# Seven block products in place of eight for the gate and up matrices of a decoder step's feed-forward layers

## The reference, cut to what matters

```python
def swiglu(x, w_gate, w_up, w_down):
    return (jax.nn.silu(x @ w_gate) * (x @ w_up)) @ w_down
...
f1 = swiglu(rmsnorm(x, W['ffn1_pre_g'][l]), W['ffn1_w_gate'][l], W['ffn1_w_up'][l], W['ffn1_w_down'][l])
x = x + 0.5 * rmsnorm(f1, W['ffn1_post_g'][l])
```

## Time and profile before

| | us |
|---|---|
| median of 3 runs | 1166.08 |
| lowest, highest | 1164.78, 1174.18 |
| span of the profiled execution, first to last instruction | 1167.8 |
| its PE busy | 1120.6 |
| its DVE busy | 615.3 |
| its ACT busy | 329.2 |
| its POOL busy | 42.9 |

### The profile page before, as it was taken

How to read it: one execution, slowest core, us unless ns; L and a number is a source line. 1 busy time by engine, 2 the same in 40 slices (tenths; PEclk the granted TensorE clock), 3 DMA queues, 4 the chain that set the end, 5 groups by cost and what they waited for, 6 DMA issues and landing times. The chain is left out here.

```text
span 1167.8 us, 22671 instructions
## 1 busy us (share of the span) xinstructions
PE 1120.6 (96%) x9522; PEld 1097.9 (94%) x9522; DVE 615.3 (53%) x1015; ACT 329.2 (28%) x496; POOL 42.9 (4%) x57
## 2 busy tenths in 40 slices
PE   6999999999999999999899989999999999999996
PEld 6999999999999999999777789999999999999996
DVE  5534344323434778788869637873434333243446
ACT  5321222112222334331234433442122221122221
POOL 0000000000000000030223000000000000000001
PEclk9999999999999979999779989899999999999998
DMA  6322323222232221232601002213232322222222
GB/s 216 95 80 90 108 72 103 78 90 91 72 108 72 73 86 38 63 88 60 96 2 39 2 1 93 73 41 95 77 113 72 108 72 90 90 82 98 72 73 77
DMA packets 35394, 91.99 MB, mean 79 GB/s; under 512 B 10368, under 2 KB 12928, under 8 KB 35328
## 3 DMA queue, kind: packets, MB, share of 16 engines
q1 hardware_dynamic: 34320, 88.78, 25.0%
q10 hardware_dynamic: 1008, 2.27, 0.6%
HBM read 87.76 MB, written 3.28 MB: 78 GB/s over the span
## 5 line engine op out<-in xcount | busy, mean ns | idle before, releaser
L306 PE MATMUL ps<-xh,wh 128*128 128x272 f32 x1840 | 404.0, 293 | 16.4 <-DVE xl L503 8.6
L306 PE MATMUL ps<-xh,wl 128*128 128x272 f32 x1840 | 400.3, 291 | 0.0
L306 PE MATMUL ps<-xl,wh 128*128 128x272 f32 x1840 | 399.3, 290 | 0.0
L306 PEld LDWEIGHTS ps<-xh,wh 128*128 128x128 f32 x1840 | 299.3, 191 | 19.0 <-DVE wl L289 9.0
L306 PEld LDWEIGHTS ps<-xl,wh 128*128 128x128 f32 x1840 | 299.6, 191 | 0.0
L306 PEld LDWEIGHTS ps<-xh,wl 128*128 128x128 f32 x1840 | 297.7, 191 | 0.0
L284 ACT ACTIVATE wh<-raw 128x1024 fp32r<-128x1024 f32 (+1 forms) x163 | 168.1, 1034 | 324.6 <-PE ps L306 208.6
L289 DVE TENSOR_TENSOR wl<-raw,wh 128x1024 fp32r<-128x1024 f32 (+1 forms) x163 | 192.8, 1203 | 38.0 <-ACT wh L284 37.7
L306 PE MATMUL ps<-hh,wh 128*128 128x272 f32 x704 | 157.7, 290 | 0.0
L306 PE MATMUL ps<-hh,wl 128*128 128x272 f32 x704 | 156.7, 290 | 0.0
L306 PE MATMUL ps<-hl,wh 128*128 128x272 f32 x704 | 156.5, 289 | 0.0
(11 more groups left out here) (312 smaller groups left out, 790.3 us busy)
## 6 DMA issues: line engine op xcount, KB each, us to landing
raw<-in_w_gu SPq DMA_DIRECT2D x88, 512.0 KB, 3.6
raw<-in_w_d SPq DMA_DIRECT2D x32, 512.0 KB, 3.6
raw<-in_w_in SPq DMA_DIRECT2D x19, 512.0 KB, 3.6
raw<-in_w_d SPq DMA_DIRECT2D x16, 384.0 KB, 3.0
raw<-in_w_out SPq DMA_DIRECT2D x8, 512.0 KB, 3.6
out_y<-x SPq DMA_DIRECT2D x16, 136.0 KB, 1.7
x<-in_x ACTq DMA_DIRECT2D x4, 272.0 KB, 5.6
x<-in_x SPq DMA_DIRECT2D x4, 272.0 KB, 6.7
```

The lines of the kernel that those rows point to most:

```text
L306: last = pe.matmul(out[:, n], left[:, s, j], right[:, j, n * H:n * H + H], start=first and opens and j == order[0], stop=final and closes ...
```

## The change

In groups 1 and 2 of both feed-forward layers (16 of the 22 hidden tiles in each) the gate and up units of a hidden tile are replaced by seven block products. The weights of a tile are taken as a 2 x 2 matrix of blocks (gate and up, by first and second half of the contraction), the input as another (first and second half of the contraction, by first and second half of the tokens). Of a 2 x 2 block product, seven products of sums of blocks do instead of eight (the Winograd form). Each of the seven is 4 x 3 = 12 matmuls of 272 columns.

What is added around them:

- Per feed-forward layer, during the down product of group 0: for four pairs of input tiles, ACT copies them times the norm's gain (`rows_act`, two of 544 columns), GpSimd makes four sums of 272 columns (`ffn_pool`), ACT and DVE split these into `seven` (`rows_hi_act`, `rows_lo_dve`, 1088 columns each).
- Per hidden tile: GpSimd makes four sums of weight blocks of 512 columns (`fast_pool`), in the columns of `xh` and `xl` that the seven products don't read. ACT and DVE split seven blocks instead of four half tiles' worth of two units (`fast_hi`, `fast_lo`: three of 512 columns and two of 1024). The products add up in three PSUM banks of 272 columns; between them ACT copies a partial sum out four times (`fast_copy`), and the next product adds on in the same bank. DVE joins the parts with three additions of 272 columns (`fast_first`, `fast_gate`), multiplies by `rb`, and after silu multiplies twice by 272 columns (`fast_hidden`); the hidden tile's split is as before.
- A second load buffer `raw2` holds the odd tiles; a tile's two loads (gate and up) are issued together, when the tile two before it is split.

The same 2 x 512 KB per hidden tile are loaded. Group 0, the down products and the mixer keep their instructions; the counters of both layers are merged and the units renumbered.

```diff
+        seven = at("ffn", "seven", [2, 4, 4, H], F32R, offset=TB)
+        raw2 = at("ffn", "raw2", [2, KD, P], offset=TB + 32 * 4 * H)
...
+        def fast_sp(sp, q, g, u):
+            f0, nf = GROUPS[g]
+            with sp.Fori(0, nf // 2) as i:
+                for s in range(2):
+                    sp.wait_ge(S("f_lo"), i * 10 + (5 * (16 * q + f0 - FAST0 + s) + 5))
+                    if s:
+                        sp.wait_ge(S("q_lo"), 4 * q + 4)
+                    else:
+                        sp.wait_ge(S("w_lo"), u + RAW)
+                    for k in range(2):
...
+                        sp.dma_start(fast_raw(s, k).rearrange("p k n -> p (k n)"), src).then_inc(S(f"f_raw{s}"), 16)
+
+        def fast_pool(pool, q, g):
...
+                    landed(pool, q, g, i, s)
+                    pool.wait_ge(S("f_lo"), i * 10 + (5 * n + 7))
+                    pool.tensor_tensor(sum_(0), up[:, 0:4], up[:, 4:8], ADD).then_inc(S("f_sum"), 1)
+                    pool.wait_ge(S("f_sum"), i * 8 + (16 * q + 16 + 4 * n + 1))
+                    pool.tensor_tensor(sum_(1), sum_(0), gate[:, 0:4], SUB).then_inc(S("f_sum"), 1)
+                    pool.wait_ge(S("f_lo"), i * 10 + (5 * n + 9))
+                    pool.tensor_tensor(sum_(2), gate[:, 0:4], up[:, 0:4], SUB).then_inc(S("f_sum"), 1)
+                    pool.wait_ge(S("f_sum"), i * 8 + (16 * q + 16 + 4 * n + 2))
+                    pool.tensor_tensor(sum_(3), gate[:, 4:8], sum_(1), SUB).then_inc(S("f_sum"), 1)
...
+        def fast_pe(pe, q, g, i, s, dn):
...
+            for m, (high, low) in enumerate(rights):
+                pe.wait_ge(S("f_lo"), i * 10 + (10 + 5 * n + (1, 2, 2, 3, 4, 4, 5)[m]))
+                if m == 1:
+                    pe.wait_ge(S("q_lo"), 4 * q + 4)
+                if m in (2, 4, 5, 6):
+                    pe.wait_ge(S("f_copy"), i * 8 + (4 * n + {2: 1, 4: 3, 5: 2, 6: 4}[m]))
+                out = fast_bank(s, (0, 1, 0, 2, 0, 1, 0)[m])
+                hi, lo_ = slots(wh, m), slots(wl, m)
+                for j in range(4):
+                    for left, right in ((hi, high), (hi, low), (lo_, high)):
+                        last = pe.matmul(out, left[:, j], right[:, j], start=m in (0, 1, 3) and j == 0 and left is hi and right is high,
+                                         stop=j == 3 and left is lo_, skip_group_check=True)
+                last.then_inc(S("f_done"), 1)
...
+        def fast_gate(dve, q, g, i, s):
...
+            dve.tensor_tensor(h32[:, s % 2, H:N], h32[:, s % 2, H:N], five[s % 2][:], ADD).then_inc(S("f_part"), 1)
+            dve.wait_ge(S("f_done"), i * 14 + (7 * (n + 1) + 6))
+            dve.tensor_tensor(silu[:, s % 2, H:N], fast_bank(s, 1), silu[:, s % 2, H:N], ADD).then_inc(S("f_part"), 1)
+            dve.wait_ge(S("f_part"), i * 6 + (3 * n + 3))
+            dve.tensor_tensor(silu[:, s % 2], silu[:, s % 2], rb[:], MUL).then_inc(S("gate"), 1)
+
+        def fast_hidden(dve, q, g, i, s):
...
+            dve.tensor_tensor(h32[:, s % 2, H:N], silu[:, s % 2, H:N], h32[:, s % 2, H:N], MUL)
...
+            dve.tensor_tensor(h32[:, s % 2, 0:H], silu[:, s % 2, 0:H], fast_bank(s, 0), MUL).then_inc(S("h_mul"), 1)
+            hidden_split_dve(dve, q, i, f0, s)
+
+        def fast_tile_act(act, q, g, i, s):
+            fast_copy(act, q, g, i, s, 0)
+            fast_hi(act, q, g, i, s + 1, 0)
+            fast_copy(act, q, g, i, s, 1)
+            fast_copy(act, q, g, i, s, 2)
+            fast_hi(act, q, g, i, s + 1, 1)
+            fast_hi(act, q, g, i, s + 1, 2)
+            fast_copy(act, q, g, i, s, 3)
+            fast_hi(act, q, g, i, s + 1, 3)
+            silu_act(act, q, i, GROUPS[g][0], s)
+            fast_hi(act, q, g, i, s + 1, 4)
+
+        def fast_tile_dve(dve, q, g, i, s):
+            fast_lo(dve, q, g, i, s + 1, 0)
+            fast_lo(dve, q, g, i, s + 1, 1)
+            fast_first(dve, q, g, i, s)
+            fast_lo(dve, q, g, i, s + 1, 2)
+            fast_gate(dve, q, g, i, s)
+            fast_lo(dve, q, g, i, s + 1, 3)
+            fast_hidden(dve, q, g, i, s)
+            fast_lo(dve, q, g, i, s + 1, 4)
...
+                pool.tensor_tensor(qq[:, 0], b12, b11, SUB).then_inc(done, 1)
+                pool.tensor_tensor(qq[:, 2], b22, b12, SUB).then_inc(done, 1)
...
                 for s in range(KD):
...
                     split_hi(act, u, 0, s, nf)
                     if s == 1:
                         silu_act(act, q, 0, f0, nf - 1)
...
+                    if s % 2 == 0:
+                        if s:
+                            rows_hi_act(act, q, s // 2 - 1)
+                        rows_act(act, q, s // 2)
+                rows_hi_act(act, q, 3)
```

More of the change, by code:

```diff
@@ L262, in program @@
         block = ctx.enter_context(nc.Block())
-        FFN_UNITS = sum(2 * nf + KD for _, nf in GROUPS)
+        FFN_UNITS = 2 * GROUPS[0][1] + KD * len(GROUPS)
         MIX0 = FFN_UNITS
@@ L713, in final_pool, with fast_raw, slots, two @@
                 pool.tensor_tensor(x[:, k, part_of(1)], x[:, k, part_of(1)], tb3[:, k % 3, part_of(1)], ADD).then_inc(S("y_pool"), 1)
+        FAST0 = GROUPS[1][0]
+        def fast_raw(s, k):
+            return (raw2 if s % 2 else raw)[:, k]
+        def slots(w, first, count=1):
+            return w[:].rearrange("p s k n -> p (s k) n")[:, 4 * first:4 * (first + count)]
+        def two(t):
+            return t.rearrange("p (s k) n -> p s k n", s=2)
+        def sum_(n):
+            return sums[n // 2][:, :, H + P * (n % 2):H + P * (n % 2) + P]
@@ new lines, in fast_pool @@
+        def fast_pool(pool, q, g):
+            f0, nf = GROUPS[g]
+            with pool.Fori(0, nf // 2) as i:
+                for s in range(2):
+                    n = 16 * q + f0 - FAST0 + s
+                    gate, up = fast_raw(s, 0), fast_raw(s, 1)
+                    landed(pool, q, g, i, s)
[7 more added lines that the diff above has]
+                    pool.tensor_tensor(sum_(3), gate[:, 4:8], sum_(1), SUB).then_inc(S("f_sum"), 1)
@@ new lines, in fast_hi @@
+        def fast_hi(act, q, g, i, s, k, u=None):
+            n = 16 * q + GROUPS[g][0] - FAST0 + s
+            if k in (1, 3):
+                act.wait_ge(S("f_sum"), i * 8 + (16 * q + 16 + 4 * n + k + 1))
+            else:
+                landed(act, q, g, i, s)
+            act.wait_ge(S("f_done"), i * 14 + (7 * n + (1, 3, 4, 6, 7)[k]))
+            if u is not None:
+                act.wait_ge(S("unit_done"), SPL + u - 4 + (1, 2, 2, 3, 4)[k])
+            act.activation(left_to(wh, k), left_of(s, k), ACT.Copy).then_inc(S("f_hi"), 1)
@@ new lines, in fast_copy @@
+        def fast_copy(act, q, g, i, s, k):
+            f0 = GROUPS[g][0]
+            n = 16 * q + f0 - FAST0 + s
+            act.wait_ge(S("f_done"), i * 14 + (7 * (n + 1) + (1, 2, 3, 5)[k]))
+            if k == 0:
+                act.wait_ge(S("h_mul"), i * 2 + (FT * q + f0 + s + 1))
+            if k == 3:
+                act.wait_ge(S("h_lo"), i * 2 + (FT * q + f0 + s + 1))
+            to = (silu[:, s % 2, 0:H], five[s % 2][:], silu[:, s % 2, H:N], h32[:, s % 2, H:N])[k]
+            act.activation(to, fast_bank(s, (0, 1, 0, 0)[k]), ACT.Copy).then_inc(S("f_copy"), 1)
@@ new lines, in slots_free, with fast_act @@
+        def slots_free(act, q, g, s):
+            f0, nf = GROUPS[g]
+            act.wait_ge(S("f_done"), 7 * (16 * q + f0 - FAST0 + nf) + (2, 4, 6, 7)[s])
+            act.wait_ge(S("h_mul"), FT * q + f0 + nf - 1 + 1)
+        def fast_act(act, q, g, u):
+            f0, nf = GROUPS[g]
+            for k in range(5):
+                fast_hi(act, q, g, 0, 0, k, u)
+            with act.Fori(0, nf // 2 - 1) as i:
+                for s in range(2):
+                    fast_tile_act(act, q, g, i, s)
+            fast_tile_act(act, q, g, nf // 2 - 1, 0)
+            end = (q, g, nf // 2 - 1, 1)
+            fast_copy(act, *end, 0)
+            fast_copy(act, *end, 1)
+            for d in range(4):
+                if d in (1, 2):
+                    fast_copy(act, *end, d + 1)
+                if d == 3:
+                    silu_act(act, q, nf // 2 - 1, f0, 1)
+                slots_free(act, q, g, d)
+                split_hi(act, u, 0, d, nf)
@@ new lines, in fast_dve @@
+        def fast_dve(dve, q, g, u, n):
+            f0, nf = GROUPS[g]
+            for k, d in enumerate((4, 5, None, 6, 7)):
+                fast_lo(dve, q, g, 0, 0, k)
+                if d and (g > 1 or d > 5):
+                    down_dve(dve, q, u - KD, g - 1, d, n)
+            with dve.Fori(0, nf // 2 - 1) as i:
+                for s in range(2):
+                    fast_tile_dve(dve, q, g, i, s)
+            fast_tile_dve(dve, q, g, nf // 2 - 1, 0)
+            end = (q, g, nf // 2 - 1, 1)
+            split_lo(dve, u, 0, 0, nf)
+            fast_first(dve, *end)
+            split_lo(dve, u, 0, 1, nf)
+            fast_gate(dve, *end)
+            split_lo(dve, u, 0, 2, nf)
+            fast_hidden(dve, *end)
```

(25 more changed lines are left out.)

185 lines of the change are left out of this document (137 added, 48 removed).

## The result

| | before | after |
|---|---|---|
| median (lowest to highest), 17 runs each, us | 1174.16 (1164.78 to 1179.81) | 1162.69 (1153.68 to 1166.33) |
| ratio, 95% interval | | 0.9907, 0.9886 to 0.9929 |
| span of the profiled execution | 1167.8 | 1152.4 |
| feed-forward stages, groups 1 and 2 of the first layer, then of the second | 96.2, 96.2, 96.2, 96.2 | 95.5, 88.6, 95.3, 88.7 |

The account below looks back on a forecast made before the run. PE was taken as the bound, the number of matmuls setting the stages' time. 1167.8 - 47.4 saved + 6 of standing PE = 1126.4 against the profiled span, 1.7 above the runs' median: 1125 us, range 1117 to 1154.

Parts of the forecast that it names:

- Matmuls: 32 hidden tiles go from 96 to 84 matmuls, 12.03 to 10.55 us each, saving 47.4 us (46.4 to 48.3).
- the lower of the two ends: New hidden tile on PE: 10.52 us at the 0.1252 pitch, the other end 10.58 at 0.1259.
- The price of a sum: Hidden tiles: each 512-column GpSimd sum costs DVE 0.85 us (0 to 1.13), on top of 8.3 a tile alone.
- the bounds given: GpSimd's weight sums were to take 1.1 to 1.9 us each, stretched by turns with DVE.
- The group's budget: Eight-tile group: DVE needs 86.8 us beside PE's 84.4; PE stands 1.5 per group, 6 in all (0 to 32).
- the cushion: Within a tile's chain of gate, silu and copy, DVE may be 1.2 us late before PE stands.
- The input sums: Beside group 0's down units: 27 us of work hidden, counted as nothing; uncovered, at most some 10 us twice.
- The sum: Whole kernel: 1167.8 - 47.4 + 6 = 1126.4 against the profiled span, so 1125 us.
- A: Rival, the port: GpSimd and DVE hardly overlap, 24 tiles with sums take 11.2 to 12.8 us; 1154 us, chance 0.21.
- C: Rival, the copies: products wait for ACT to empty their PSUM bank, 19 us lost; 1144 us, chance 0.12.
- B: Rival, the clock: PE stands in each of 24 tiles and its clock falls; 1177 to 1226, named 1195 us, chance 0.06.

Follow-up runs that it names:

- e5: Changed kernel with DVE instead of GpSimd making the weight sums, and DVE's input-sum low parts moved ahead of down outputs: 1132.09 us, 0.9645 of before.
- e1: Changed kernel with GpSimd's weight sums cut from 512 columns to one, except in group 1's first two tiles: 1141.82 us, 0.9746 of before.
- e3: Changed kernel with DVE's low parts of the input sums moved ahead of the down outputs in group 0: 1153.3 us, 0.9843 of before.
- e6: Changed kernel with one-column weight sums (except group 1's first two tiles) plus four unread 512-column GpSimd sums per tile: 1195.51 us, 1.0201 of before.
- e4: Changed kernel with a tile's first PSUM copy on ACT moved ahead of the previous tile's silu and last split: 1159.72 us, 0.9872 of before.

## Why the prediction was wrong

**Matmuls, right.** 9138 of them; without waits a tile takes 10.50 us (e5), just under the lower of the two ends, so twelve matmuls into one bank cost nothing beyond the pitch.

**The price of a sum, right.** A tile of DVE was put at 8.3 alone and 0.85 a sum, 11.7 with four; it measures 11.62. The two terms are off by a little, in opposite directions: alone it is 8.04 (e5), so a sum costs (11.62 - 8.04) / 4 = 0.9. That 8.3 and 0.85 give nearly the same total is luck. The stretched operations say the same: 1.11 lost by the 272 columns, 0.50 by the cast, 0.88 by `hl`, 1.08 by the two low parts (2.37 against 1.29 in e1), 3.57 in all. POOL's sums take 1.35 to 1.69 us on the mean, in the bounds given. One thing I had left out: the cast, too, is held up, 0.94 beside GpSimd against 0.44. The Trainium skill, SBUF — State Buffer, section "Who interferes with whom", names casts among the operations that can take the ports shared with GpSimd, in their two-port modes. The trace agrees that the cast is held up (0.94 against 0.44); in which mode it ran, no run shows.

**The group's budget, wrong.** "DVE then needs 8 x 8.3 + 24 x 0.85 = 86.8 us beside PE's 84.4", and from this "1.5 us of standing PE per group". The sum over eight tiles lets a tile without sums pay for one with them. It can't: DVE waits for splits, and so for copies of PE's products, in a light tile as well, and what it idles there is lost. During the first tile of group 2, when GpSimd's sums for it and the next were long made, DVE stood for 2.65 us:

```profile
272.18 1.23 DVE L806 TENSOR_TENSOR wl<-sums,wh 128x1024 fp32r<-128x1024 f32 x1 [2.65 <-ACT wh L801]
```

Six tiles late by 11.62 - 10.50 = 1.1 are 6.7 us; the cushion takes about two of them, and PE stands in four tiles of group 2: 88.6 - 84.1 = 4.5, three times the 1.5. In group 1, with the start mended (e3), it is 90.0 - 84.1 = 5.9. There the premise fails too that tiles 0 and 1 have their sums outside the stage: it begins at 123, and GpSimd's sums of tile 1 at 128.96 (124.74 in e3). Together 20.9 us in four stages instead of 6.

**The input sums, wrong.** "I count nothing" rested on the room in ACT's and DVE's time beside the down units. The room is there: e3 and e5 hide them. But four steps over two shared buffers pass ACT, GpSimd, ACT and DVE in turn, and three of the four turns on DVE stood behind a down output. The price had been named, "at most some 10 us twice"; it measured 5.5 and 5.3, the latter with some 1.4 of slow clock (see the rivals).

**The sum.** PE stands for 20.9 + 10.8 = 31.7 us in place of 6, and a tile at 10.50 instead of 10.55 gives 1.6 back, 24.1 together: the stages miss by 41.4 - 16.7 = 24.7, of which 0.5 is the way they are counted. Of 1162.7 - 1125 = 37.7, a further 8.1 is the higher median of before, and the rest, some 5, is gain that the medians don't show: 16.7 in the stages against 11.5 between the medians (8.3 to 13.4 by the interval). It must lie outside the stages, where the stretch between the layers is longer in seven of eight profiles with the new code. As a whole it varies too much to tell, by 12.5 us between the changed kernel's own two profiles, but its last part repeats: from PE's wait for `mixf` at the end of the mixer to the start of group 0's down product it is 164.0 and 164.2 us in the two profiles of before, 168.6 and 170.0 in the two of after, and 168.2 to 173.1 in e1 to e6. These 4.6 and 5.8 us are about the gain that is missing. They go with the new code; by what means is open, beyond the slow clock shown at the end, 3.3 of the 4.6.

**The rivals.** A was the mechanism, and its tile of 11.2 to 12.8 holds the 11.62; but PE lost it in 18 tiles (five in each group 1, four in each group 2), not 24, which is 18 x 1.1 = 20 us. "Two tiles of eight have no sums", the reason against A, was true of group 2 only and worth less than I gave it. C had the right place and the wrong cause (e4). B did not come in the loop: the waits of 0.8 us a tile left the clock at 1.00 (from 160 to 210 and from 280 to 350 us). At the start of group 1 the 2.31 us of the first layer left it at 1.00 as well; behind the 2.18 of the second it fell, busy time by stretch after:

```profile
860.00:864.00 4.00, 3.92 (x21) 3.60 (x21) 3.36 (x2) 1.65 (x3) 3.92 (x3) 0.61 0.54 217
```

21 matmuls where 32 fit, 11 x 0.125 = 1.4 us, once in this profile.

## What to carry to other kernels

Work moved to a helper engine is not free for the loaded one: here four sums of 512 columns cost DVE some 0.9 us each on GpSimd, as both read SBUF, and 0.63 when DVE made them, so the sums belonged on DVE. Where two engines hand to each other in every tile, compare them tile by tile, since idle time in one tile does not pay for the next. Work that fits beside another stage by its amount is hidden only if its place in each engine's order lets its chain run; a chain of steps that share their buffers is to be laid out step by step.

## What the runs showed of the hardware that was not expected

DVE's cast, with one SBUF input, is held up beside GpSimd like the two-input operations: 843 ns on the mean of 28 in the changed kernel and 1243 in e6, against 444 in e5, where GpSimd is idle.

The clock can make the same 8 us of work cost different times from one kernel to the next. Behind the hand-over to the second feed-forward layer, after the same wait of PE (0.63 us), the stretch holds 66 matmuls at a clock of 1.00 before, 40 at 0.57 after, and in e6, whose code there is the changed kernel's, 65 at 1.00 again. The second profile of before has 65 at 1.00; e1 to e5 and the second of after have 36 to 40 at 0.51 to 0.57. Busy time by stretch, before, after and e6:

```profile
753.57:761.57 8.00, 8.00 (x66) 8.00 (x66) 6.49 (x21) 2.68 (x6) 0.00 (x0) 1.00 0.23 68
```

```profile
744.27:752.27 8.00, 8.00 (x40) 8.00 (x41) 5.41 (x18) 2.15 (x5) 0.00 (x0) 0.57 0.22 67
```

```profile
769.25:777.25 8.00, 8.00 (x65) 8.00 (x66) 6.49 (x21) 2.68 (x6) 0.00 (x0) 1.00 0.23 69
```

26 matmuls of 0.125 are 3.3 us. What decides it I did not find; the instructions are the same.
